# Three later RMS norms: the reciprocal root applied behind the products, and high and low parts made of the weighted stream tile by tile

## The reference, cut to what matters

```
a = rmsnorm(h, norm_mix);  mix = [mLSTM(a @ w_in), S5(a @ w_in)] ;  h = h + mix @ w_out
c = rmsnorm(h, norm_ffn)                       # norm 1
q = c @ w_q                                    # queries; top 16 of two key sets, 16 experts per head
act = gelu(sum_d peer_u[idx] * c) * softmax(scores);   h = h + act @ peer_v[idx]
gate = sigmoid(rmsnorm(h, norm_ple) @ w_ple_gate)      # norm 2
h = h + (p @ w_ple_proj) * gate
y = rmsnorm(h, norm_final)                     # norm 3
rmsnorm(x, g) = x * rsqrt(mean(x*x, over columns) + 1e-6) * g
```

## Time and profile before

| | |
|---|---|
| time, median of 3 runs | 2318.35 us (2316.54 to 2325.18) |
| time of the profiled execution | 2317.02 us |
| its span in the profile | 2315.5 us |
| share of the span that PE, DVE, ACT, POOL are busy | 69%, 79%, 38%, 36% |

### The profile page before, as it was taken

The page is one execution under the profiler, slowest core; times in us unless marked ns, Lnnn a source line. Parts: engine busy times, 40 slices in busy tenths (PEclk is TensorE's granted clock), DMA queues, the critical chain, the costliest instruction groups (busy, mean ns, idle before and its releaser), DMA issues. The chain is left out here.

```text
span 2315.5 us, 25341 instructions
## 1 busy us (share of the span) xinstructions
PE 1590.7 (69%) x8027; PEld 1301.0 (56%) x8027; DVE 1821.1 (79%) x2819; ACT 870.9 (38%) x1500; POOL 840.2 (36%) x593
## 2 busy tenths in 40 slices
PE   8999999889977000000222215899999999999897
PEld 6777777658977000000221214777777777776796
DVE  4587863576665999998899975788888888888666
ACT  3200004213344121222877753444444444444443
POOL 0000000000001787888777768533433444443000
PEclk9999999778987555555555558999999999999898
DMA  7234444335544999999999990799999999998353
GB/s 208 77 117 137 145 127 139 100 113 164 163 109 160 408 412 408 406 422 407 402 416 402 421 420 20 268 347 353 352 341 347 349 344 346 352 341 284 111 165 98
DMA packets 257308, 619.56 MB, mean 268 GB/s; under 512 B 28436, under 2 KB 174484, under 8 KB 215444
## 3 DMA queue, kind: packets, MB, share of 16 engines
q0 software_dynamic: 56320, 369.13, 39.8%
q1 hardware_dynamic: 200916, 249.62, 33.1%
HBM read 606.56 MB, written 12.13 MB: 267 GB/s over the span
## 5 line engine op out<-in xcount | busy, mean ns | idle before, releaser
L1453 ACT CAST v_high<-ring 128x1024 fp32r<-128x1024 f32 x256 | 269.1, 1052 | 369.8 <-DMA ring<-in_peer_v 198.2
L1616 DVE TENSOR_TENSOR v_low<-ring,v_high 128x1024 fp32r<-128x1024 f32 x256 | 309.2, 1223 | 60.2 <-ACT v_high L1453 58.6
L264 PE MATMUL ps<-low,ring 128*128 128x288 f32 x1280 | 313.7, 408 | 4.4 <-DMA ring<-in_w_in 3.4
L1297 PE MATMUL ps<-v_high,act_h 128*128 128x512 f32 x896 | 296.7, 401 | 18.7 <-ACT v_high L1453 18.0
L1297 PE MATMUL ps<-v_high,act_l 128*128 128x512 f32 x896 | 292.2, 396 | 0.0
L264 PEld LDWEIGHTS ps<-low,ring 128*128 128x128 f32 x1280 | 244.3, 191 | 72.6 <-issue 4.9
L1153 POOL DMA_INDIRECT ring<-in_peer_u,work x128 | 124.7, 975 | 428.2 <-DVE work L1520 372.6
L1272 PE MATMUL ps<-work 128*128 128x128 f32 x512 | 105.0, 369 | 234.8 <-ACT work L1401 214.2
L1302 PE MATMUL ps<-v_low,act_h 128*128 128x512 f32 x896 | 255.5, 401 | 13.8 <-DVE v_low L1616 13.2
L1280 PE MATMUL ps<-ident,work 128*128 128x128 f32 x6 | 1.8, 437 | 376.0 <-DVE work L1538 376.0
L1474 DVE CUSTOM_DVE_ANT_0 ring<-ring,ps 128x2048 f32<-128x2048 f32 x100 | 227.3, 2278 | 25.9 <-DMA ring<-in_peer_u,work 25.3
(11 more groups left out here) (415 smaller groups left out, 3649.7 us busy)
## 6 DMA issues: line engine op xcount, KB each, us to landing
ring<-in_peer_v SPq DMA_DIRECT2D x256, 512.0 KB, 6.7
ring<-in_w_in SPq DMA_DIRECT2D x20, 2048.0 KB, 8.3
ring<-in_w_out SPq DMA_DIRECT2D x16, 1024.0 KB, 5.9
ring<-in_w_ple_gate SPq DMA_DIRECT2D x16, 1024.0 KB, 5.8
out<-work SPq DMA_DIRECT2D x37, 256.0 KB, 3.2
work<-in_state_mlstm_C SPq DMA_DIRECT2D x32, 256.0 KB, 4.8
ring<-in_peer_w_q SPq DMA_DIRECT2D x8, 1024.0 KB, 5.5
ring<-in_w_glu SPq DMA_DIRECT2D x4, 1024.0 KB, 5.2
```

Of the source, the lines that this page charges most:

```text
L264: m = pe.matmul(ps[2 * s + c][:, 0:T], ring[:, s, k * WB + c * P:k * WB + (c + 1) * P], rhs[:, k, :], start=(k == 0), stop=(k == kt - 1))
L1297: pe.matmul(ps[4 * i + 2 * hf + c], a, vh[:, hf, 512 * c:512 * c + 512], start=first and a is a_h, stop=False)
L1453: o.do(act.copy(vh[:, hf, :], natural[b % 2][:, 1024 * hf:1024 * hf + 1024]), sem("vh_done"))
L1616: o.do(v.tensor_tensor(vl[:, hf, :], natural[b % 2][:, 1024 * hf:1024 * hf + 1024], vh[:, hf, :].bitcast(F32), ALU.subtract), sem("vl_done"))
```

## The change

Each of the three norms is taken apart. The weight of the column is applied to `h` as soon as a tile of it is there, and the high and low parts are made of `h * weight`, without the root. The root is computed beside the product's first tile and multiplied in behind it.

Norm 1: `add`, the evacuation of an `out` tile on DVE, also makes the low part; ACT makes the high part (`ffn_high`). The matmul with ones (`pe_sum`) goes between the second and the third quarter of `wq`'s first tile. The evacuation of `wq` moves from ACT to DVE and multiplies with the root. The tokens that meet the gathered rows stay without the root, so the root also goes into the gelu, as a factor of each row: six matmuls with a one turn it into columns (`rcol`). Norm 2: ACT makes high parts as `pv_added` comes, DVE the low parts behind it; the squares go between ACT's copies of `embed`, which gets a third bank; DVE sums them; `pe_sum` stands in `gate`'s first tile. Every `gate` tile gets one more DVE instruction (`scaled`, which multiplies with the root). Norm 3: ACT weights each finished tile (`hg`) during `gate`; the turned groups start from these; sum, root and Newton step are done on columns of one number for each row, and the copies out multiply with them. Some tiles in `work` move to other addresses.

```diff
-        def pe_norm(pe, n):
-            for q in range(4):
-                pe.wait_ge(sem("sq_done"), 2 * n + q + 1)
-                for k in range(4 * q, 4 * q + 4):
-                    m = pe.matmul(ps[7][:, 0:T], ones[:], nT[:, k, :], start=(k == 0), stop=(k == KD - 1))
-            m.then_inc(sem("ss_done"), 1)
+        def pe_sum(pe, n):
+            if n == 1:
+                pe.wait_ge(sem("acc_done"), KD)
+            else:
+                pe.wait_ge(sem("sq0_sum"), 2)
             pe.matmul(ps[7][:, 0:T], ones[:], nT[:, 0, :], start=True, stop=True).then_inc(sem("ss_done"), 1)
+        def act_root(act, n):
+            o_act.do(act.activation(warm[:], ones[:, 0:1], ACT.Sqrt))
+            act.wait_ge(sem("ms_ready"), n + 1)
+            o_act.do(act.activation(rstd[:], rs[:], ACT.Sqrt), sem("sd_ready"))
+        def dve_root(v, o, n):
+            v.wait_ge(sem("ss_done"), n + 1)
+            o.do(v.tensor_scalar(rs[:], ps[7][:, 0:T], 1.0 / D, EPS, ALU.mult, ALU.add), sem("ms_ready"))
+            v.wait_ge(sem("sd_ready"), n + 1)
+            newton(v, o, rstd[:], rs[:], gel[:, 0, :])
...
+            if q == 2 and isinstance(i, int) and (i, c) == (0, 0) and name in NORM_OF:
+                pe_sum(pe, NORM_OF[name])
...
             pe.wait_ge(sem("key_copied"), 2)
             pe.wait_ge(sem("tile_freed"), sum(TRIPLE["wq"]))
+            for i, (t0, n) in enumerate(TOK):
+                for r in range(4 if i == 2 else 1):
+                    m = pe.matmul(ps[6][TS * r:TS * r + n, i:i + 1], rstd[0:1, t0:t0 + n], ones[0:1, 0:1], start=True, stop=True)
+            m.then_inc(sem("cols_done"), 1)
...
-                o.do(act.activation(val[:, COLS[i]], val[:, COLS[i]], ACT.Gelu_apprx_tanh), sem("act_gates"))
+                o.do(act.activation(val[:, COLS[i]], val[:, COLS[i]], ACT.Gelu_apprx_tanh, scale=rcol[:, i:i + 1]),
+                     sem("act_gates"))
...
+            def copy_q(i, c, s):
+                v.wait_ge(sem("q_used"), i * 8 + 4 * (TRIPLE["wq"][0] + c + 1))
+                o.do(v.tensor_tensor(work[:, ds(i * (2 * T) + c * T, T)], ps[4 + s][:, 0:T], rstd[:], ALU.mult),
+                     sem("tile_freed"))
...
-            pe_norm(pe, 2)
...
-                        m = pe.matmul(ps[4 + c % 2][:, 0:T], proj[:, k, c * P:(c + 1) * P], pT[:, k, :],
+                        m = pe.matmul(ps[4 + c % 3][:, 0:T], proj[:, k, c * P:(c + 1) * P], pT[:, k, :],
...
-            pe_norm_summed(pe, 3)
...
-                    m = pe.transpose(ps[g % 4][0:n, j * P:(j + 1) * P], nT[:, 4 * q + j, t0:t0 + n], ident[:])
+                    m = pe.transpose(ps[g % 4][0:n, j * P:(j + 1) * P], eT[:, 4 * q + j, t0:t0 + n], ident[:])
                 m.then_inc(sem("yt_done"), 1)
+                if g == 2:
+                    pe.wait_ge(sem("acc_done"), 2 * KD)
+                    for i2, (t2, n2) in enumerate(TOK):
+                        m = pe.matmul(ps[7][0:n2, i2:i2 + 1], nT[:, 0, t2:t2 + n2], ones[:, 0:1], start=True, stop=True)
+                    m.then_inc(sem("ss_done"), 1)
...
         def act_tail(act, o):
+            for k in range(KD):
+                act.wait_ge(sem("pv_added"), k + 1)
+                o.do(act.activation(ple_h[:, k, :], hT[:, k, :], ACT.Copy, scale=gv[:, 32 + k:33 + k]), sem("n_high"))
...
+                o.do(act.copy(eT[:, c, :], ps[4 + c % 3][:, 0:T]), sem("e_copied"))
+                if c % 3 == 2 and c < 12:
+                    q = c // 3
+                    o.do(act.activation(nT[:, 4 * q:4 * q + 4, :], hT[:, 4 * q:4 * q + 4, :], ACT.Square), sem("sq_done"))
+            act_root(act, 2)
+            def hg(i, c):
+                act.wait_ge(sem("h_added"), i * 2 + (c + 1))
+                o.do(act.activation(work[:, ds(i * (2 * T) + (14336 + c * T), T)], low[:, ds(i * (2 * T) + c * T, T)], ACT.Copy,
+                                    scale=gv[:, ds(i * 2 + (48 + c), 1)]), sem("hg_ready"))
             def sig(i, c, s):
-                act.wait_ge(sem("q_used"), i * 8 + 4 * (b + c + 1))
-                o.do(act.activation(sg[:, s, :], ps[4 + s][:, 0:T], ACT.Sigmoid), sem("sig_done"))
+                act.wait_ge(sem("tile_freed"), i * 2 + (TRIPLE["gate"][0] + c + 1))
+                o.do(act.activation(sg[:, s, :], sg[:, s, :], ACT.Sigmoid), sem("sig_done"))
+                if not (isinstance(i, int) and (i, c) == (0, 0)):
+                    hg(i, c - 1)
...
+            def scaled(i, c, s):
+                v.wait_ge(sem("q_used"), i * 8 + 4 * (TRIPLE["gate"][0] + c + 1))
+                o.do(v.tensor_tensor(sg[:, s, :], ps[4 + s][:, 0:T], rstd[:], ALU.mult), sem("tile_freed"))
+                if not (isinstance(i, int) and (i, c) == (0, 0)):
+                    gated(i, c - 1, 1 - s)
...
+            gated(KD // 2 - 1, 1, 1)
+            v.wait_ge(sem("ss_done"), 4)
+            o.do(v.tensor_scalar(x3[:, 0:2], ps[7][:, 0:2], 1.0 / D, EPS, ALU.mult, ALU.add))
+            o.do(v.tensor_scalar(x3[0:TS, 2:3], ps[7][0:TS, 2:3], 1.0 / D, EPS, ALU.mult, ALU.add), sem("ms_ready"))
...
+            newton(v, o, f3, x3, t3, sem("r3_ready"))
...
-            pe_norm_summed(pe, 1)
...
+            def ffn_high(i, c, s):
+                act.wait_ge(sem("tile_freed"), i * 2 + (c + 1))
+                o.do(act.activation(ffn_h[:, ds(i * 2 + c, 1), :], low[:, ds(i * (2 * T) + c * T, T)].unsqueeze(1), ACT.Copy,
+                                    scale=gv[:, ds(i * 2 + (16 + c), 1)]), sem("n_high"))
+            high_parts(act, o, "out", ffn_high, {"n_high": 2}, ahead=True)
             high_parts(act, o, "wq", None, {}, only_first=True)
-            act_norm(act, 1)
-            act_norm_high(act, o, 1, ffn_h)
+            act_root(act, 1)
...
                 squares(i, c, s)
+                v.wait_ge(sem("n_high"), i * 2 + (c + 1))
+                o.do(v.scalar_tensor_tensor(ffn_l[:, ds(i * 2 + c, 1), :], h.unsqueeze(1), gv[:, ds(i * 2 + (16 + c), 1)],
+                                            ffn_h[:, ds(i * 2 + c, 1), :].bitcast(F32), ALU.mult, ALU.subtract),
+                     sem("n_ready"))
+            low_parts(v, o, "out", None, add, {"tile_freed": 2, "n_ready": 2}, ahead=True)
             low_parts(v, o, "wq", None, None, {}, only_first=True)
-            dve_norm(v, o, 1, ffn_h, ffn_l)
+            dve_root(v, o, 1)
```

More of the change, by code:

```diff
@@ L284, in pe_linear, with newton @@
                 blk(i, 1, False)
[L287 to L328, removed]
+        def newton(v, o, r, x, t, done=None):
             o.settle()
@@ L336, in newton @@
             o.settle()
-            o.do(v.scalar_tensor_tensor(r, t, 1.5, r, ALU.add, ALU.mult))
+            o.do(v.scalar_tensor_tensor(r, t, 1.5, r, ALU.add, ALU.mult), done)
             o.settle()
@@ L1326, in act_peer @@
         def act_peer(act, o):
[L1327 to L1331, removed]
+            high_parts(act, o, "wq", None, {}, ahead=True)
             o.do(act.copy(identr, ident[:]), sem("ffn_copied"))
@@ L1409, in act_peer @@
             sums(0, 64)
+            act.wait_ge(sem("rcol_ready"), 1)
             softmax_exp(0, 4)
@@ L1712, in act_tail @@
                 o.do(act.copy(pT[:, c, :], ps[c][:, 0:T]), sem("pt_copied") if c else None)
-            act.wait_ge(sem("pv_added"), 16)
-            act_norm(act, 2, lambda: high_parts(act, o, "gate", None, {}, only_first=True))
-            def copy_e(c):
+            high_parts(act, o, "gate", None, {}, only_first=True)
+            for c in range(KD):
                 act.wait_ge(sem("e_done"), c + 1)
-                o.do(act.copy(eT[:, c, :], ps[4 + c % 2][:, 0:T]), sem("e_copied"))
-            act_norm_high(act, o, 2, ple_h, copy_e)
+                o.do(act.copy(eT[:, c, :], ps[4 + c % 3][:, 0:T]), sem("e_copied"))
[7 more added lines that the diff above has]
+                                    scale=gv[:, ds(i * 2 + (48 + c), 1)]), sem("hg_ready"))
             def sig(i, c, s):
-                b = TRIPLE["gate"][0]
-                act.wait_ge(sem("q_used"), i * 8 + 4 * (b + c + 1))
-                o.do(act.activation(sg[:, s, :], ps[4 + s][:, 0:T], ACT.Sigmoid), sem("sig_done"))
+                act.wait_ge(sem("tile_freed"), i * 2 + (TRIPLE["gate"][0] + c + 1))
+                o.do(act.activation(sg[:, s, :], sg[:, s, :], ACT.Sigmoid), sem("sig_done"))
+                if not (isinstance(i, int) and (i, c) == (0, 0)):
+                    hg(i, c - 1)
             o.open = {}
-            high_parts(act, o, "gate", sig, {"sig_done": 2}, ahead=True)
-            act_norm(act, 3)
+            high_parts(act, o, "gate", sig, {"sig_done": 2, "hg_ready": 2}, ahead=True)
+            hg(KD // 2 - 1, 1)
+            o_act.do(act.activation(warm[:], ones[:, 0:1], ACT.Sqrt))
+            act.wait_ge(sem("ms_ready"), 4)
+            o.do(act.activation(f3, x3, ACT.Sqrt), sem("sd_ready"))
+            act.wait_ge(sem("r3_ready"), 1)
             for g in range(0, 12, 2):
@@ L1732, in act_tail @@
```

(39 more changed lines are left out.)

47 lines of the change are left out of this document (27 added, 20 removed).

## The result

The changed kernel takes 2293.8 us (median of 4 runs, 2293.0 to 2296.7) beside 2317.4 for the kernel before on the same chip; the ratio is 0.9894, 95% interval 0.987 to 0.9918. That is faster, by 23.6 us where 27.6 were forecast, and inside the range.

A forecast was written before the change was run, and what follows sets the result against it. No engine's share was taken as the bound: PE bounds the products, DMA the gathers, a DVE and ACT chain the norms. Gains 11.7 + 8.15 + 7.75 = 27.6 us off 2317.0 give 2289.4, said as 2290; range 2283 to 2301.

The forecast's parts named there:

- Norm 1: From the end of `out` to the first gather: keys 12.6 us earlier, less 0.9, gives 11.7 us.
- Norm 2: From the experts' sum through `gate`: `gate` starts 11.0 us earlier, less 0.5 + 2.35 in its first tile, gives 8.15 us.
- Norm 3: From the last `gate` matmul to the span's end: 17.7 us instead of 25.45, a gain of 7.75 us.
- The start of `wq`: Behind `out`: `wq` starts 2.7 us after the end of `out`, with DVE later than ACT.
- the stall: Behind the first tile of `wq` and of `gate`: PE waits 2.35 us, as DVE does the root before low parts.
- the matmul with ones: Inserted in the first tile of `wq` and of `gate`: two passes at 0.248 us, 0.5 us in all.
- The columns of the root: Before the scores: six added matmuls of one column cost 0.9 us, bounds 0 and 2.8.
- The gathers: Expert stage after the scores: DMA-bound as before, the whole stage starts and ends 11.7 us earlier.
- `embed` starts at the landing of w_ple_proj: In norm 2: this transfer is late next, landing at 2158.2, 12.9 us after its issue.
- The ring of DVE and ACT: Rival, chance 0.05: in `out` and `gate` the engines' turns bound each tile; at 7.3 us a tile, 28 us lost.
- the gathers swallowed nothing: Answers a rival, chance 0.05: the gather stage ends where it ended, norm 1's gain is lost, 2302 us.
- The clock's rival: Chance 0.18: three new PE waits, before `wq`, in `wq` and in `gate`, lower the clock; 5.5 to 13.5 us lost.

The follow-up runs named there:

- the versions above: Follow-up runs of edited versions of the changed kernel, ratios 0.9836 to 0.9945; in the old order w_ple_proj's transfer comes behind the two tiles of w_ple_gate.
- the first profile: Profiled execution of the changed kernel from its first measurement, against the kernel before: 2293.8 us, ratio 0.9894.
- second profile: The changed kernel run once more with no further edit, against the kernel before: 2297.18 us, ratio 0.9891.

## Why the prediction was right, and where it was off

*Norm 1.* Near in each term but one. Forecast 12.6 us until the keys; 11.40 came, of which 0.37 were there before `out` ended, so 11.03. The start of `wq` and the stall were within 0.15 us; the matmul with ones cost 0.7 (7.13 us for the first tile, where 48 matmuls at 0.1336 are 6.41) and not 0.5. What was left out is the clock's fall behind `out`, 1.5 us in this execution; 12.55 with it given back. The columns of the root cost 0.70 where 0.9 were put down.

*The gathers.* That the stage passes norm 1's gain on whole holds only within what the stage wanders by itself. In twelve profiled executions it took from 1406.2 to 1420.3 us: 1410.7 and 1412.7 with norm 1 as before, 1413.7 on the average of the ten others. The 1.6 us that the changed kernel lost there are inside that spread; no run shows a cause for them, and none excludes that norm 1 costs a us or two there.

*Norm 2.* `gate` started 11.17 us earlier, counted from the experts' sum, for 11.0. That `embed` starts at the landing of w_ple_proj held in both profiles of the changed kernel, and so the transfer was the next thing late, as the prediction said; in two of the versions above, with the old order of the transfers, ACT's copy came last by a little (0.79 and 0.80 us of waiting). Its distance to ACT's copy is small when the sum of the experts is turned at half clock (1.42 us of waiting) and large when it is not (5.37).

*`gate`.* Forecast 2.85 us longer than before, measured 4.26. The stall was 2.03 instead of 2.35; the matmul with ones cost 0.7 and not 0.5; the fall behind the stall, 1.5 us, was not in the sum.

*Norm 3.* 17.3 us behind the last matmul for 17.7, so 8.1 instead of 7.75 us. Part of this agreement is luck: the root was there after 6.4 us for 7.0, the copies then took 7.5 for 6.75, and from the last copy to the end it was 3.4 for 3.96.

*The rivals.* The ring of DVE and ACT did not bind, and the gathers swallowed nothing that can be shown. The clock's rival was true at two of the three places in the first profile. The step that failed is the one that argued it away: "in `embed` the clock stayed at the upper level over 2.90 us of waiting". Its row, 2172, lies inside the wait, where the clock reads 1.00 ahead of a fall too (643 and 2174 in the profile after). That it held there is shown by the stretch behind the wait:

```profile
2174.00:2187.00 13.00, 12.88 (x52) 9.80 (x52) 12.50 (x29) 9.97 (x28) 0.00 (x0) 1.00 0.00 1
```

One such stretch shows that a wait may pass, not that it does: behind 2.03 us in `gate` the clock fell in 4 of 4 executions, behind 2.56 us ahead of `wq` in 2 of 7, behind 2.30 us in `wq` in 1 of 5. The length of the wait alone does not decide: 2.90 us in `embed` passed in both profiles that have it, 2.93 us in norm 3 in none of ten. The section of the Trainium skill that the prediction cites for this rival ("TensorE: Matmul & The Clock Gate", "Why this matters for your kernels") advises only against longer gaps than the three that were forecast, so it was no support for the rival; these counts are. The rival's price was too high as well: 1.5 us a fall, where it put 1.85 to 4.5, so it cost 3.0 us and not 5.5 or more.

Clock (3.0) and the wander of the experts (1.6), less 1.1 us of terms that came out better (0.37 before norm 1, 0.15 columns and scores, 0.17 norm 2, 0.39 norm 3), are the 3.5 us between 27.6 and 24.1. Shown by experiment are the clock's share in `gate`, by filling the wait, and the origin of the stalls; the fall behind `out` is priced by two executions of one program. Why it came in some executions and not in others stays open, and so does the cause of the 1.6 us.

## What to carry to other kernels

A root that only scales rows can go behind the product, and PE need not wait for it; then look for the next chain on the engine that makes the product's operands, here the root itself, queued ahead of the second tile's low parts. Start that chain as early as its input allows: moving one matmul by two quarters took the stall away. Short waits that replace a long one cost more than their length where the clock falls behind them (1.5 us a fall here); price them, and look at the clock behind the wait, not in it. Where nothing else is there to run, a few matmuls without a reader can hold the clock: it held over each of the four waits filled here, though only in `gate` had it fallen each time without them. And compare executions only in the same state of the clock: a fall somewhere else can hide or feign what an edit gains.

## What was not expected of the hardware

A DVE reciprocal of 288 columns takes 1.95 to 1.96 us, where the other instructions of that size take 0.46; on 3 columns it is 0.18:

```profile
2279.68 0.18 DVE L298 RECIPROCAL work<-work 128x3 f32<-128x3 f32 x1 [0.34 <-ACT work L1728]
```

It is the longest link of the root's chain, and a reason to do the root on columns, as norm 3 now does.

The stretch in which the experts' sum is turned takes 9.6 us at the upper level of the clock (2136.0 to 2145.57, second profile) and 13.1 when the clock falls in it (2133.16 to 2146.23, first); it fell in six of the twelve profiles. In the changed kernel it is hidden: `embed` starts 15.9 and 15.8 us behind the start of that stretch in the two, since it waits for w_ple_proj.
